# First expert's rows gathered in the other order, down weights one place later in the queue, and three weight places in the second layer's experts

## What is computed

```python
def moe(x, router_w, router_b, w_gate, w_up, w_down):
    probs = jax.nn.softmax(logits, axis=-1)
    ...                                   # best group of experts, top 2 inside it, weights comb
    hid = jax.nn.silu(jnp.einsum('bld,edf->blef', x, w_gate)) * jnp.einsum('bld,edf->blef', x, w_up)
    hid = hid * comb[..., None].astype(hid.dtype)
    return jnp.einsum('blef,efd->bld', hid, w_down)

for layer in range(DEPTH):
    h = _layer_norm(DN_ALPHA * h + mix, p['ln_mix_g'][layer], p['ln_mix_b'][layer])
    ffn = moe(h, p['router_w'], p['router_b'], p['moe_w_gate'][layer], p['moe_w_up'][layer], p['moe_w_down'][layer])
    h = _layer_norm(DN_ALPHA * h + ffn, p['ln_ffn_g'][layer], p['ln_ffn_b'][layer])
```

## Time and profile before

| | us |
|---|---|
| median of 3 runs | 997.81 |
| lowest, highest | 995.53, 1002.62 |
| the profiled execution, timed whole | 997.95 |
| its span in the profile | 996.2 |
| TensorE busy | 931.0 (93%) |
| VectorE busy | 396.7 (40%) |
| mean granted TensorE clock | 0.956 |

### The profile page before, as it was taken

The page is one execution under the profiler, slowest core; times in us unless marked ns, Lnnn a source line. Parts: engine busy times, 40 slices in busy tenths (PEclk is TensorE's granted clock), DMA queues, the critical chain, the costliest instruction groups (busy, mean ns, idle before and its releaser), DMA issues.

```text
span 996.2 us, 12551 instructions
## 1 busy us (share of the span) xinstructions
PE 931.0 (93%) x5078; PEld 514.4 (52%) x5078; DVE 396.7 (40%) x820; ACT 177.5 (18%) x314; POOL 215.4 (22%) x322
## 2 busy tenths in 40 slices
PE   8999988998999999999889879899989999999993
PEld 5888867986365433333333368744454333333331
DVE  4599517726635112222224279502642121221115
ACT  0402131223020101111001243301301111111011
POOL 4679982301020511111000110100201101111000
PEclk9999997999997999999999999999879999999997
DMA  9446739102769599999999926760589789999982
GB/s 270 107 153 246 256 131 303 63 12 99 264 212 403 208 401 404 404 413 396 409 405 425 417 58 187 229 247 1 203 354 337 303 352 408 396 416 398 417 338 87
DMA packets 83419, 277.27 MB, mean 278 GB/s; under 512 B 25240, under 2 KB 44134, under 8 KB 60694
## 3 DMA queue, kind: packets, MB, share of 16 engines
q1 hardware_dynamic: 70298, 255.86, 66.8%
q10 hardware_dynamic: 10660, 16.49, 5.2%
q0 software_dynamic: 2400, 4.07, 1.4%
HBM read 260.97 MB, written 18.01 MB: 280 GB/s over the span
## 4 chain that ended last, share of the span: by engine, by line
PE 77%; DMA 11%; DVE 7%; ACT 2%; issue 1%; SPq 0%; DVEq 0%; ACTq 0%
PE ps L1814 19%; PE ps L342 11%; DMA ring<-in_moe_w_up 11%; PE ps L1838 9%; PE ps L2491 6%; PE ps L1856 5%; PE ps L1781 3%; PE ps L804 3%; PE ps L1793 2%; PE ps L2353 1%; PE ps L305 1%; PE ps L1480 1%; PE ps L633 1%; PE ps L650 1%; PE ps L2368 1%
## 5 line engine op out<-in xcount | busy, mean ns | idle before, releaser
L1814 PE MATMUL ps<-ring,work 128*64 128x512 f32 x480 | 217.7, 606 | 11.1 <-DMA ring<-in_moe_w_up 9.7
L1815 PE MATMUL ps<-ring,work 128*64 128x512 f32 x480 | 217.9, 607 | 0.0
L1814 PEld LDWEIGHTS ps<-ring,work 128*64 128x64 f32 x480 | 64.1, 139 | 138.9 <-issue 123.9
L1898 DVE TENSOR_TENSOR work<-ps,work 64x512 f32<-64x512 f32 x32 | 33.8, 1057 | 232.7 <-ACT work L1869 232.7
L1838 PE MATMUL ps<-ring,work 128*64 128x512 f32 x248 | 113.0, 598 | 2.7 <-DVE work L1903 1.4
L342 PE MATMUL ps<-work,ring 128*128 128x264 f32 x512 | 115.2, 387 | 0.0
L1839 PE MATMUL ps<-ring,work 128*64 128x512 f32 x248 | 113.1, 599 | 0.0
L342 PEld LDWEIGHTS ps<-work,ring 128*128 128x128 f32 x512 | 96.9, 190 | 16.3
L1249 POOL TENSOR_TENSOR ring<-ring 128x512 f32<-128x512 f32 (+5 forms) x76 | 90.4, 1207 | 9.5 <-DVE ring L1245 6.2
L1908 DVE COPY work<-ps 64x512 f32<-64x512 f32 x32 | 22.2, 693 | 151.1 <-PE ps L1839 151.1
L1919 POOL COPY work<-work 64x1 int32<-64x1 int32 x30 | 5.4, 179 | 311.9 <-PE ps L1781 275.2
(11 more groups left out here) (487 smaller groups left out, 1216.2 us busy)
## 6 DMA issues: line engine op xcount, KB each, us to landing
ring<-in_moe_w_down SPq DMA_DIRECT2D x31, 2048.0 KB, 16.8
ring<-in_moe_w_gate SPq DMA_DIRECT2D x60, 1024.0 KB, 14.7
ring<-in_moe_w_up SPq DMA_DIRECT2D x60, 1024.0 KB, 16.8
ring<-in_w_in ACTq DMA_DIRECT2D x6, 2048.0 KB, 9.1
s_out_mats<-ring SPq DMA_DIRECT2D x4, 1280.0 KB, 4.7
ring<-in_w_in SPq DMA_DIRECT2D x2, 2048.0 KB, 10.3
s_in_mats<-ring SPq DMA_DIRECT2D x4, 1024.0 KB, 6.3
ring<-in_w_out SPq DMA_DIRECT2D x1, 4096.0 KB, 16.4
```

Source lines behind the costliest of these rows:

```text
L1814: nc.tensor.matmul(ps[0:SLOT, 5, :], xgT[s][:, c], gate_w[slot][:, c], start=c == 0, stop=c == DC - 1)
L1815: last = nc.tensor.matmul(ps[SLOT:P, 5, :], xgT[s][:, c], up_w[slot][:, c], start=c == 0, stop=c == DC - 1)
L1898: nc.vector.tensor_tensor(hid[s][0:SLOT].rearrange("t (c p) -> t p c", c=4), strided(ps[SLOT:P, 5, :]), strided(sg[s][SLOT:P]), ALU.mult). ...
```

## The change

Three edits.

1. The first expert's rows. The one-hot is now the stationary operand and `xperm` the moving one, 512 columns at a time: 3 tiles times 2 halves, 6 matmuls in place of 24. The result is rows, not transposed; ScalarE and VectorE copy one half each into `first_rows`, and TensorE then transposes them with `to_features` as it does for every other expert. `first_rows` is the first half of `ypair[0]`, which lies in the memory of `xperm`; both copies therefore wait until `x_rows` has landed. The 6 matmuls stand ahead of the lists' matmuls on TensorE, and VectorE makes `first_slot` ahead of `in_list`.
2. In both layers the down weights are issued one expert later in the queue, up to expert 8; at expert 9 two down loads stand together, and from expert 10 on the order is as before.
3. In layer 1, gate, up and down use all three places in turn for all experts, and each load waits for the expert three before it.

```diff
-            for c in range(DC):
-                for i in range(3):
-                    n = tok(i)
-                    last = nc.tensor.matmul(ps[:, 4, c * SLOT:(c + 1) * SLOT], xperm[0:n, i, c * P:(c + 1) * P], first_slot[0:n, i, 0],
+            for i in range(3):
+                n = tok(i)
+                for half in range(2):
+                    last = nc.tensor.matmul(ps[SLOT * half:SLOT * half + SLOT, 7, :], first_slot[0:n, i, 0], xperm[0:n, i, 512 * half:512 * half + 512],
                                             start=i == 0, stop=i == 2)
-            last.then_inc(sem(f"tokens_done{l}"), 1)
+            last.then_inc(*pe.done(f"{tag}first_rows"))
+
+        def act_first_rows(a, tag, l):
+
+            a.wait_ge(sem(f"x_rows{l}"), 48)
+            a.wait_ge(*pe.at(f"{tag}first_rows"))
+            nc.scalar.copy(first_rows[:, 0:512], ps[0:SLOT, 7, :]).then_inc(*ac.done(f"{tag}first_rows"))
+
+        def dve_first_rows(v, tag, l):
+
+            v.wait_ge(sem(f"x_rows{l}"), 48)
+            v.wait_ge(*pe.at(f"{tag}first_rows"))
+            nc.vector.tensor_copy(first_rows[:, 512:D], ps[SLOT:P, 7, :]).then_inc(*dv.done(f"{tag}first_rows"))
+
+        def pe_first_tokens(t, tag, l):
+
+            t.wait_ge(*ac.at(f"{tag}first_rows"))
+            t.wait_ge(*dv.at(f"{tag}first_rows"))
+            to_features(ps[:, 4], first_rows, DC, sem(f"tokens_done{l}"))
...
-            return three(k, u, s)
+            return round_of_three(k, u, s) if l == 1 else three(k, u, s)
...
-            return three(k, u, s) if l == 1 else (s, u + 1)
-
-        def before_last(k):
-
-            return k - 2 if isinstance(k, int) and k < 5 else k - 1
+            return round_of_three(k, u, s) if l == 1 else (s, u + 1)
+
+        def round_of_three(k, u, s):
+
+            return (k % 3, k // 3 + 1) if isinstance(k, int) else (s, u - 1 - s)
+
+        def before_last(l, k):
+
+            if not isinstance(k, int):
+                return k - 1 + l
+            return k - 2 if k < 5 or l == 1 else k - 1
...
                 gate_up_load(q, l, *load_of(k))
-                if (l, k) != (1, 3):
-                    down_load(q, l, *load_of(k - 1))
+                if (l, k) in ((0, 3), (1, 3), (1, 4)):
+                    continue
+                for d in (k - 2, k - 1) if k == 9 else (k - 2 if k < 9 else k - 1,):
+                    down_load(q, l, *load_of(d))
```

More of the change, by code:

```diff
@@ L1548, in route_pe @@
             keep_busy(0, 2)
+            pe_first_rows(t, tag)
             t.wait_ge(*dv.at(f"{tag}lists"))
@@ L1664, in route_dve @@
             nc.vector.tensor_tensor(at_slot, iota80[:, 0:SLOT].unsqueeze(1).to_broadcast([P, 6, SLOT]), of(0, SLOT), ALU.is_equal).then_inc(*dv.done())
+            in_first = rt(0, 48)[:, 3:9]
+            nc.vector.tensor_scalar(in_first, at[:, 1].rearrange("p i j -> p (i j)"), 0.0, None, ALU.is_equal).then_inc(*dv.done())
+            v.wait_ge(*dv.last())
+            nc.vector.tensor_tensor(first_slots, at_slot, in_first.unsqueeze(2).to_broadcast([P, 6, SLOT]), ALU.mult).then_inc(*dv.done())
+            v.wait_ge(*dv.last())
+            nc.vector.tensor_tensor(first_slot[:, :, 0], first_slot[:, :, 0], first_slot[:, :, 1], ALU.add).then_inc(*dv.done(f"{tag}first_slot"))
             nc.vector.tensor_tensor(in_list, iota80.unsqueeze(1).to_broadcast([P, 6, LISTS]), of(1, LISTS), ALU.is_equal).then_inc(*dv.done())
@@ L1668, in route_dve @@
             nc.vector.tensor_tensor(list_value, in_list, per_list(value_f), ALU.mult).then_inc(*dv.done(f"{tag}lists"))
-            nc.vector.tensor_tensor(first_slots, at_slot,
-                                    in_list[:, :, 0:1].to_broadcast([P, 6, SLOT]), ALU.mult).then_inc(*dv.done())
-            v.wait_ge(*dv.last())
-            nc.vector.tensor_tensor(first_slot[:, :, 0], first_slot[:, :, 0], first_slot[:, :, 1], ALU.add).then_inc(*dv.done(f"{tag}first_slot"))
+            dve_first_rows(v, tag, 0 if tag == "n0" else 1)
             weight, both = rt(6, 3, 2), rt(0, 48)[:, 0:3]
@@ L1761, in gate_up_load @@
                 if not first(k):
-                    waits(q, l)(freed, before_last(k))
+                    waits(q, l)(freed, before_last(l, k))
                 cols = slice(half * 4 * FF, (half + 1) * 4 * FF)
@@ L1771, in down_load @@
             if l == 1 and not first(k):
-                waits(q, l)("down_done", before_last(k))
+                waits(q, l)("down_done", before_last(l, k))
             if l == 0 and late(k):
@@ L1783, in to_features, with pe_first_rows @@
             last.then_inc(signal, 1)
-        def pe_first_tokens(t, tag, l):
+        first_rows = ypair[0][0:SLOT]
+        def pe_first_rows(t, tag):
             for i in range(3):
@@ L2003, in moe_act @@
         def moe_act(a, tag, l):
+            act_first_rows(a, tag, l)
             act_tokens(a, l, *at_expert(0))
```

## The result

| | before | after |
|---|---|---|
| median, 11 runs each (us) | 999.34 | 991.96 |
| lowest, highest | 994.88, 1002.86 | 988.03, 996.03 |
| ratio, 95% interval | | 0.9929, 0.991 to 0.9948 |
| the profiled execution, timed whole | 997.95 | 988.86 |
| its span | 996.2 | 987.1 |

The change makes the kernel 7.1 us faster (5.2 to 9.0), less than 1%. The forecast was 5.4 us. The 999.34 is the median of 11 runs of the kernel before; the forecast started from three of them, with 997.81.

The account below looks back on a forecast made before the run. TensorE, busy 93% of the span, was taken as the chain, with its waits and slow work what pays. Layer 0's +1.4 and layer 1's -6.8 gave -5.4 on 997.95, forecast 992.5 us, range 988 to 996 (985 to 999 with partial rivals).

Parts of the forecast that it names:

- The sum: Whole kernel: +1.4 us in layer 0 and -6.8 in layer 1, together -5.4, giving 992.5 us.
- Edit 1, layer 0: New first rows in layer 0: expert 0's earlier start, with the low clock counted, gains 1.3 us, bounds 0.9 to 3.2.
- the chain behind x_rows: From x_rows' release to expert 0's gate and up: copy, transposes, copy to xgT and two signals, 2.35 us.
- the case that the forecast priced at 0.9: Layer 0, expert 0: low clock lasts until 325.2 us despite the earlier start, so 0.9 us of gain is kept.
- the middle of two cases: Layer 0: 1.3 us, between 1.8 (low clock equally long from the start) and 0.9 (low until 325.2 us).
- Edit 1, layer 1: New first rows in layer 1: expert 0's gate and up start 3.1 us earlier, all kept; bounds 1.6 to 4.5.
- the forecast of +1.4: Layer 0's net change: 2.7 us later from the queue less 1.3 from the first rows, +1.4 us.
- Edit 2: Layer 0's queue: the DMA engines' dry time moves and grows, making the stream 2.7 us later; bounds 1 to 4.
- rival 3: Layer 0's late down loads: waits at experts 5 and 7 add, clock falls behind each; total +4.0, 1002 us; chance 0.06.
- Edit 3: Layer 1's third place: the 2.03 us weight wait and 1.7 us of low clock go, -3.7 us; bounds -2.0 to -3.7.
- Rival 2: Layer 1's third place pays nothing, or copies delay the first gather; total -1.7 to -0.5 us; chance 0.14.
- Rival 1: Layer 0's new queue order fills the dry time, its 7.7 us of waits go; total -15.8, 982.1 us; chance 0.12.

Follow-up runs that it names:

- e1: Kernel before with only the new first rows, queue and places as before; -1.3 us (-3.6 to +1.0) by the medians.
- e4: Changed kernel with layer 0's queue as before the change; median 992.62 us, by the ratios 3.3 us slower than the changed kernel.
- e7: Changed kernel with layer 0's down loads of experts 2 and 3 together behind expert 4's gate and up; layer 0's last down 3.75 us sooner, total not given.
- e2: Kernel before with only layer 0's down loads one expert later in the queue; +2.8 us (-0.1 to +5.8).
- e3: Kernel before with only layer 1's three places in turn and its new queue order; -1.9 us (-4.0 to +0.3).
- e5: Changed kernel with the x_rows store ahead of expert 1's gate and up loads in both layers; by the ratios 4.1 us faster than the changed kernel.
- e6: Changed kernel with 3 unused 128x512 matmuls in the idle gap ahead of the first rows' transposes; by the ratios 5.3 us faster than the changed kernel.
- e9: Changed kernel with early x_rows store and layer 0's down loads of experts 2 and 3 together at expert 4; layer 0's last down at 261.8 us, total not given.
- e8: Changed kernel with early x_rows store and layer 0's queue as before the change; 982.0 us, ratio 0.9816 to the kernel before.
- e11: Repeat of e8, the changed kernel with early x_rows store and layer 0's old queue; 983.77 us, ratio 0.9866 to the kernel before.
- e10: Changed kernel with early x_rows store, layer 0's old queue, and VectorE making the gathers' indices first; median 984.48 us.
- e12: Changed kernel with early x_rows store, layer 0's two down loads together at expert 4, and gather indices first; ratio 0.9793 (0.9769 to 0.9816) to the kernel before.

## Why the prediction came out

**The sum** was -5.4; the medians gave -7.1 (-9.0 to -5.2) and the changed stretches of the profile -5.7. The time, 991.96 against 992.5, is partly luck: the kernel before had a median of 999.3 over 11 runs and not 997.8, and the parts below miss in both directions.

**Edit 1, layer 0: forecast 1.3, measured 0.6, outside the bounds of 0.9 to 3.2.** Expert 0's gate and up start 1.07 us sooner, where the forecast had 1.8, and then take 8.92 us, where they took 8.44; expert 1's start 0.59 us sooner. Two steps failed. The first is the chain behind x_rows, 2.35 us by the forecast and 2.92 in both layers (316.07 to 318.99): the transposes took 1.40 us where I took 0.87 from a row at full clock, though the next paragraph of the forecast has TensorE come out of its idle time at 1.2 GHz. x_rows also released 0.2 us later than before, from the end of mixer 0. The second is how long the low clock lasts. It ended 35.3 us behind mixer 0 (323.0 us), before 35.4 (325.2): the case that the forecast priced at 0.9, while I took the middle of two cases. Measured from expert 1's start the other kernels give about the same: 45.7 to 45.9 us behind the mixer in e1, e4 and e7, against 46.6 and 46.1 in e2 and e3 (before 46.6, after 46.0), so the 0.6 itself is uncertain by some 0.5.

**Edit 1, layer 1: forecast 3.1, measured 2.9.** The same 0.57 us was lost, and x_rows released 0.4 us sooner, which no step had. The low clock ended 2.9 us sooner with the start (739.5 us, before 745.1), gate and up took 8.32 us against 8.29, and expert 1's start 2.92 us sooner.

**What edit 1 cost and the forecast had at nothing.** The idle time ahead of layer 0's last combine was 2.1 to 2.6 us in the three kernels without edit 1 and 3.5 to 3.9 in the eleven with it. The copies that it needs end 0.6 to 0.8 us behind the last down in all of them, so it isn't these; the trace names no releaser, and the cause is open. With the 0.35 us at the output this is some 1.5 us. Layer 0's change of +0.75 came near the forecast of +1.4 only because the clock on that combine gave 1.7 back.

**Edit 2: +2.7 forecast, +2.4 and +2.15 measured** (the last down, after against e1 and e4), +1.0 in e2. Every step is in the trace of SP after the change; with the 2.1 us by which this execution is ahead, the three issues that the forecast timed, expert 4's, 5's and 6's, stand at 339.5, 363.4 and 382.0 us against 340.0, 364.0 and 382.6:

```profile
337.42 0.33 SPq L1775 DMA_DIRECT2D ring<-in_moe_w_gate  x1
...
361.34 0.33 SPq L1775 DMA_DIRECT2D ring<-in_moe_w_gate  x1
...
379.94 0.33 SPq L1775 DMA_DIRECT2D ring<-in_moe_w_gate  x1
```

What the sum of dry times left out are some 2 us at 320 to 330 us, in both kernels, which cancel. The dry time grew by 1.4 to 1.8 us in the table's pairs of old and new queue (after against e1 and e4, e2 against before), forecast 2.3. The waits were 3.06 us at down of 5 and 1.70 at down of 7, forecast 2 and 4. The clock fell behind the first, as rival 3 had it, and it cost nothing at the end, as the forecast had it, since the loads set the end: the later waits shrank from 7.7 to 4.1 us.

**Edit 3: -3.7 forecast, -3.87 in e3**, -3.8 between e1 and after. The wait and the clock's fall both went. Both pairs differ in layer 1's order of the queue as well as in the third place, and no run parts the two. Rival 2 is out.

**Layer 0's account.** The table shows more than the forecast used. In all fourteen kernels layer 0's last down ends 260 us (258.8 to 261.1) behind the mixer plus the dry time, which goes from 1.9 to 13.5 us. Expert 0's start goes from 25.1 to 32.4 us in them, and beside the dry time it explains next to nothing: e5 starts expert 0 3.8 us sooner than e7 and ends 0.5 later, with 0.8 more dry time. By this account the forecast's sum for layer 0, 2.7 less 1.3 for the earlier start, adds two things of which only the dry time should count, and its +1.4 against +1.36 at the last down is partly luck too. The account's own scatter is 1.2 us to either side, so it can't decide this: e1 ends 1.0 us sooner than before with 0.2 less dry time, e6 0.5 sooner than the changed kernel with 1.5 less. Rival 1 was right about the size of the prize (e9, with the early x_rows, takes 9.6 us in layer 0) and wrong that this order takes it.

## What to carry to other kernels

Where loads set a stage's end, add up the time in which the DMA engines are dry since its start; here the stage moved by that sum to within 1.2 us over a range of 11.6, whatever single waits did, and an order of the queue is good if it leaves work for the engines during each long wait of the issuing engine. When a wait is filled, cost the work behind it at the clock that the idle time leaves, and find the next transfer whose cover is gone. For effects under 1%, compare stage by stage from a mark in unchanged code, and look for the low clock in both profiles first: the medians of the kernel before went from 996.95 to 1001.75 us between sets of 12 to 31 runs, and one kernel's two ratios (e8, e11) differed by 0.5%.

## What the runs showed of the hardware

**The same code differs by 4 us.** The end of mixer 0 lies between 287.45 and 291.58 us in the fourteen profiles, with nothing changed ahead of it. Busy time by window, before and then after, over the same matmuls (16 of L319 from 13.6 us on, 5.49 us and then 3.80) and over layer 0's last combine:

```profile
13.60:18.00 4.40, 4.32 (x12) 3.48 (x13) 4.03 (x22) 0.00 (x0) 0.36 (x1) 0.62 1.04 382
...
563.00:568.00 5.00, 4.46 (x7) 1.95 (x8) 0.00 (x0) 0.61 (x2) 2.27 (x4) 0.66 1.02 421
```

```profile
13.60:18.00 4.40, 4.40 (x27) 3.60 (x27) 4.03 (x22) 0.00 (x0) 0.64 (x1) 1.00 1.05 388
...
563.00:568.00 5.00, 4.09 (x16) 1.55 (x16) 0.00 (x0) 0.00 (x0) 2.28 (x4) 1.00 1.01 419
```

The clock was low on them in one execution and not in the other. In the four profiles without a low clock there (after, e6, e9, e11) mixer 0 ends at 287.45 to 287.72 us, in the eight with 3.4 us of it at 288.55 to 289.86, in the two with 6.8 us of it (e2, e4) at 291.37 and 291.58. Likewise on the last combine of layer 0, which follows idle time in every kernel and took 5.4 us before and 3.7 after. With it the stretch from the last down to the last combine is 7.7 to 10.7 us long in the fourteen profiles.

**Loads ran at 404 GB/s for 104 us**, and at 426 in layer 1 after the change (the window from 926 us in the section on the result). The Trainium skill (DMA: Bandwidth & Descriptors, Where 436 GB/s comes from) has loads from HBM bound at about 358 GB/s. With one core at work the rows show more, and the measurement decides.

**The output is 0.36 us later in every kernel with edit 1, but not in e10 and e12**, where two of VectorE's instructions stand elsewhere. The time is idle time ahead of one of VectorE's instructions of the last norm (0.46 us at L1435 after the change, under 0.15 before), the same code in all. Its cause is open.
